# A two-layer encoder step on one core: two sums of weight blocks moved from VectorE to accumulating DMAs

## The reference, cut to what matters

```
def swiglu(x, w_gate, w_up, w_down):
    return (jax.nn.silu(x @ w_gate) * (x @ w_up)) @ w_down
...
x = x + 0.5 * swiglu(rms_norm(x, g_norm[l, 0]), w_ffn_gate[l, 0], w_ffn_up[l, 0], w_ffn_down[l, 0])
```

## Time and profile before

| | |
|---|---|
| median of 3 runs | 2529.57 us (2527.84 to 2533.5) |
| profiled execution: its time, its span | 2533.5 us, 2531.5 us |
| PE busy | 2422.3 us |
| DVE busy | 1932.6 us |
| ACT busy | 1337.9 us |
| POOL busy | 358.6 us |
| bytes moved by DMA | 300.90 MB |

### The profile page before, as it was taken

The page is one execution under the profiler, slowest core; times in us unless marked ns, Lnnn a source line. Parts: engine busy times, 40 slices in busy tenths (PEclk is TensorE's granted clock), DMA queues, the critical chain, the costliest instruction groups (busy, mean ns, idle before and its releaser), DMA issues. The chain is left out here.

```text
span 2531.5 us, 48940 instructions
## 1 busy us (share of the span) xinstructions
PE 2422.3 (96%) x18377; PEld 2273.4 (90%) x18377; DVE 1932.6 (76%) x3856; ACT 1337.9 (53%) x2870; POOL 358.6 (14%) x275
## 2 busy tenths in 40 slices
PE   8999999999998999999999999999999999999998
PEld 8999999788678999999988899999996699999998
DVE  7988989422697899898935889888928878888875
ACT  6555556201785655555522555555618756555554
POOL 0111111244000110111034011111031000111100
PEclk9999999999999999999999999999999999999999
DMA  4445353232763343445334554544357642544432
GB/s 128 108 91 117 87 118 80 85 117 84 276 245 106 76 117 85 112 97 112 71 87 135 150 115 96 113 98 106 82 207 256 221 114 60 124 102 103 108 84 79
DMA packets 352037, 300.90 MB, mean 119 GB/s; under 512 B 18305, under 2 KB 312378, under 8 KB 351554
## 3 DMA queue, kind: packets, MB, share of 16 engines
q1 hardware_dynamic: 279376, 246.98, 31.3%
q0 software_dynamic: 65776, 32.52, 10.5%
q10 hardware_dynamic: 6658, 18.37, 2.0%
HBM read 281.69 MB, written 16.13 MB: 118 GB/s over the span
## 5 line engine op out<-in xcount | busy, mean ns | idle before, releaser
L914 PE MATMUL PS<-x_area,w_area 128*128 128x320 f32 x3096 | 485.1, 310 | 0.0
L914 PEld LDWEIGHTS PS<-x_area,w_area 128*128 128x128 f32 x3096 | 461.1, 188 | 3.1 <-ACT PS L1710 2.9
L1625 ACT ACTIVATE w_area<-R 128x512 fp32r<-128x512 f32 (+2 forms) x583 | 322.7, 567 | 184.4 <-DVE R L2290 92.0
L2263 DVE TENSOR_TENSOR w_area<-R,w_area 128x512 fp32r<-128x512 f32 (+2 forms) x583 | 354.6, 617 | 67.8 <-ACT w_area L1625 67.3
L2263 DVE TENSOR_TENSOR r_area<-R,r_area 128x512 fp32r<-128x512 f32 (+2 forms) x437 | 270.7, 620 | 111.1 <-ACT r_area L1625 101.3
L914 PE MATMUL PS<-r_area,w_area 128*128 128x320 f32 x1584 | 268.3, 313 | 20.0 <-ACT PS L1710 12.6
L1625 ACT ACTIVATE r_area<-R 128x512 fp32r<-128x512 f32 (+2 forms) x437 | 248.4, 569 | 67.4 <-DVE R L2290 39.1
L2290 DVE TENSOR_TENSOR R<-R 128x512 f32<-128x512 f32 (+2 forms) x433 | 266.9, 616 | 1.0 <-DMA R<-in_w_ffn_gate_dram 0.7
L914 PEld LDWEIGHTS PS<-r_area,w_area 128*128 128x128 f32 x1584 | 241.3, 189 | 27.0 <-ACT PS L1710 23.7
L1710 ACT ACTIVATE PS<-PS 128x320 f32<-128x320 f32 x438 | 178.2, 416 | 163.6 <-PE PS L914 151.3
L1137 PE MATMUL PS<-w_area,xn_hi 128*128 128x512 f32 x800 | 253.5, 398 | 4.8 <-POOL w_area L771 3.5
(11 more groups left out here) (338 smaller groups left out, 3955.1 us busy)
## 6 DMA issues: line engine op xcount, KB each, us to landing
R<-in_w_ffn_up_dram SPq DMA_DIRECT2D x45, 512.0 KB, 4.0
R<-in_w_ffn_gate_dram SPq DMA_DIRECT2D x43, 512.0 KB, 4.0
R<-in_w_ffn_up_dram SPq DMA_DIRECT2D x86, 256.0 KB, 3.8
R<-in_w_ffn_gate_dram SPq DMA_DIRECT2D x82, 256.0 KB, 3.9
R<-in_w_ffn_down_dram SPq DMA_DIRECT2D x52, 384.0 KB, 3.1
R<-in_w_ffn_down_dram SPq DMA_DIRECT2D x88, 192.0 KB, 3.0
vreg<-in_cache_a_v_dram SPq DMA_DIRECT2D x8, 2048.0 KB, 9.0
...
```

The source lines that it names most:

```text
L914: last = pe.matmul(PS[:, bank, 0:HT], a[:, k, :], b, start=(start and opens), stop=(k == n - 1 and a is lo), skip_group_check=True)
L1625: act.activation(role_parts(f, g, s, role)[0], role_source(f, g, s, role), ACT.Copy).then_inc(sem("early_cast") if key in EARLY_COUNT else ...
L2263: dve.tensor_tensor(lo, role_source(f, g, s, role), hi.bitcast(F32), ALU.subtract).then_inc(sem("early_split") if key in EARLY_COUNT else ...
```

## The change

S3 is made by an accumulating DMA of GpSimd: W21 from DRAM is added over W11 in place (`third_sum`), after S2's sum and W11's low part have read it. S4 of gate and up sets is made so too: W12 is added over S2 in `sums` (`fourth_sum`), after S2's low part; S4 of down sets stays on VectorE. GpSimd's order is third(at), first(then), fourth(at). The cast and the low part of S3 move from the set itself to the end of the set before. The quarters go: one load brings W11 and W21, after S3's low part of the set two before, and `first_sum` waits for it. What is not shown is the bookkeeping of counts and the removal of the first S3 sums ahead of the chains.

```diff
--- before.py
+++ after.py
...
@@ -122,8 +122,8 @@
     order = chain(f)
     out = [(order[0], role) for role in ("W11", "S1", "S2", "W12", "S3")]
     for at, then in zip(order, order[1:] + [None]):
-        out += ([(then, "W11")] if then else []) + [(at, "S4")] + ([(at, "S3")] if at != order[0] else [])
-        out += ([(then, "S1"), (then, "S2")] if then else []) + [(at, "W22")] + ([(then, "W12")] if then else [])
+        out += ([(then, "W11")] if then else []) + [(at, "S4")] + ([(then, "S1"), (then, "S2")] if then else [])
+        out += [(at, "W22")] + ([(then, "W12"), (then, "S3")] if then else [])
...
             if j in own:
@@ -204,10 +204,7 @@
             if not early:
                 self.halves[p] += 1
                 self.landed2[key] = 16 * self.halves[p]
-                parts = ((1, "S3"), (2, "W22"), (3, "S2")) if (g, s) in order else ((1, "W21"), (2, "W22"), (3, "W21"))
-                if (g, s) in order:
-                    self.landed3[key] = 16 * len(self.landed3) + 16
-                for part, last in parts:
+                for part, last in ((1, "S3" if (g, s) in order else "W21"), (2, "W22")):
                     self.raw_free[key, part] = self.raws.get((p, part), 0)
                     self.raws[p, part] = self.split[f, g, s, last]
...
 
-            def quarter_load(f, g, s):
-
-                key, p = (f, g, s), LOAD[f, g, s] % 2
-                if PLAN.raw_free[key, 3]:
-                    sp.wait_ge(w_split, PLAN.raw_free[key, 3])
-                if PLAN.landed3[key] > 16:
-                    sp.wait_ge(w_loaded3, PLAN.landed3[key] - 16)
-                sp.dma_start(role_source(*key, "S1"), weight_block(*key, 0, 1)).then_inc(w_loaded3, 16)
-                if PLAN.raw_free[key, 1]:
-                    sp.wait_ge(w_split, PLAN.raw_free[key, 1])
-                sp.dma_start(role_source(*key, "W11"), weight_block(*key, 0, 0)).then_inc(w_loaded[p], 16)
-                set_load(f, g, s, (1,))
-
             def cols(w, slot, at, kb=KB):
                 return (raw[slot][:, 0:kb * P].rearrange("p (k m) -> p k m", k=kb),
                         w[:, bass.ds(at, P)].rearrange("(k p) m -> p k m", p=P))
@@ -620,7 +603,7 @@
                     load_constants()
                 for g, s in chain(f):
                     if set_at(f, g, s) is not early:
-                        quarter_load(f, g, s)
+                        set_load(f, g, s)
...
             def add_sums(f):
 
                 def first_sum(at):
-                    key = (f, *at)
+                    key, p = (f, *at), LOAD[(f, *at)] % 2
                     if key not in PLAN.first_added:
                         return
-                    pool.wait_ge(w_loaded3, PLAN.landed3[key])
-                    if PLAN.first_added[key] > 16:
-                        pool.wait_ge(sem("first_added"), PLAN.first_added[key] - 16)
+                    pool.wait_ge(w_loaded[p], PLAN.landed[key])
+                    pool.wait_ge(sem("first_added"), PLAN.first_added[key] - 16) if PLAN.first_added[key] > 16 else None
                     pool.dma_start(role_source(*key, "S1"), weight_block(*key, 1, 1), accum_op=ALU.add).then_inc(sem("first_added"), 16)
 
+                def third_sum(at):
+                    key = (f, *at)
+                    pool.wait_ge(w_summed, PLAN.sum[(*key, "S2")])
+                    if (*key, "W11") not in EARLY_COUNT:
+                        pool.wait_ge(w_split, SPLIT[(*key, "W11")])
+                    pool.wait_ge(sem("third_added"), PLAN.third_added[key] - 16) if PLAN.third_added[key] > 16 else None
+                    pool.dma_start(role_source(*key, "S3"), weight_block(*key, 0, 1), accum_op=ALU.add).then_inc(sem("third_added"), 16)
+
+                def fourth_sum(at):
+                    key = (f, *at)
+                    if key not in PLAN.fourth_added:
+                        return
+                    if (*key, "S2") in EARLY_COUNT:
+                        pool.wait_ge(sem("early_split"), EARLY_COUNT[(*key, "S2")])
+                    else:
+                        pool.wait_ge(w_split, SPLIT[(*key, "S2")])
+                    pool.wait_ge(sem("fourth_added"), PLAN.fourth_added[key] - 16) if PLAN.fourth_added[key] > 16 else None
+                    pool.dma_start(role_source(*key, "S4"), weight_block(*key, 1, 0), accum_op=ALU.add).then_inc(sem("fourth_added"), 16)
+
                 order = chain(f)
-                for at in order:
-                    first_sum(at)
+                first_sum(order[0])
+                for at, then in zip(order, order[1:] + [None]):
+                    third_sum(at)
+                    if then is not None:
+                        first_sum(then)
+                    fourth_sum(at)
...
                     act.wait_ge(sem("first_added"), PLAN.first_added[f, g, s])
+                elif role == "S3":
+                    act.wait_ge(sem("third_added"), PLAN.third_added[f, g, s])
+                elif role == "S4":
+                    act.wait_ge(sem("fourth_added"), PLAN.fourth_added[f, g, s])
...
@@ -1774,12 +1783,12 @@
                 role_high(f, *then, "W11")
                 role_high(f, *cur, "S4")
                 hidden_rows(f, *prev, "4")
-                role_high(f, *cur, "S3")
                 role_high(f, *then, "S1")
                 copy_rows(f, *cur, 2)
                 role_high(f, *then, "S2")
                 role_high(f, *cur, "W22")
                 role_high(f, *then, "W12")
+                role_high(f, *then, "S3")
...
@@ -1802,7 +1811,6 @@
                     role_high(f, *cur, "S4")
                     if n:
                         rows_on(f, *prev, 0)
-                        role_high(f, *cur, "S3")
...
                             copy_rows(f, *then, 1)
+                        role_high(f, *then, "S3")
...
 
             def role_sum(f, g, s, role):
                 key, p = (f, g, s), LOAD[f, g, s] % 2
-                a, b = {"S1": ("S1", "W22"), "S2": ("S1", "W11"), "S3": ("S2", "W22"), "S4": ("S4", "W12")}[role]
-                if role == "S3":
-                    dve.wait_ge(w_summed, PLAN.sum[(*key, "S2")])
-                    if (*key, "W11") in EARLY_COUNT:
-                        dve.wait_ge(sem("early_split"), EARLY_COUNT[(*key, "W11")])
-                    else:
-                        dve.wait_ge(w_split, SPLIT[(*key, "W11")])
-                if role != "S2" and set_at(f, g, s) is early:
+                a, b = {"S1": ("S1", "W22"), "S2": ("S1", "W11"), "S4": ("S4", "W12")}[role]
+                if role == "S1" and set_at(f, g, s) is early:
                     dve.wait_ge(sem("early_loaded"), 32 if f == 1 else 64)
                 elif role == "S1":
-                    dve.wait_ge(w_loaded3, PLAN.landed3[key])
+                    dve.wait_ge(w_loaded[p], PLAN.landed[key])
                     dve.wait_ge(w_loaded2[p], PLAN.landed2[key])
                 elif role == "S2" and (*key, "S1") in PLAN.sum:
                     dve.wait_ge(w_summed, PLAN.sum[(*key, "S1")])
-                    if set_at(f, g, s) is not early:
-                        dve.wait_ge(w_loaded[p], PLAN.landed[key])
                 elif role == "S2":
                     dve.wait_ge(sem("first_added"), PLAN.first_added[key])
-                    dve.wait_ge(w_loaded[p], PLAN.landed[key])
                 else:
                     dve.wait_ge(w_loaded2[p], PLAN.landed2[key])
                 at = (role_source(f, g, s, x) for x in (role, a, b))
-                dve.tensor_tensor(*at, ALU.subtract if role == "S3" else ALU.add).then_inc(w_summed, 1)
+                dve.tensor_tensor(*at, ALU.add).then_inc(w_summed, 1)
...
@@ -2555,16 +2554,15 @@
                 role_low(f, *then, "W11")
                 role_low(f, *cur, "S4")
                 hidden_lows(f, *prev, "4")
-                role_low(f, *cur, "S3")
                 dve.wait_ge(w_split, SPLIT[(f, *cur, "S4")])
                 role_sum(f, *then, "S2")
                 role_low(f, *then, "S1")
                 role_low(f, *then, "S2")
-                role_sum(f, *then, "S3")
                 fifth_rows(f, *cur)
                 role_low(f, *cur, "W22")
                 first_rows(f, *cur)
                 role_low(f, *then, "W12")
+                role_low(f, *then, "S3")
...
@@ -2578,7 +2576,8 @@
                     after_up, after_gate = inner and prev[1] % 2 == 1, inner and prev[1] % 2 == 0
                     plain = (f, cur[0]) in PLAIN
                     turned = after_up and not plain
-                    role_sum(f, *cur, "S4")
+                    if is_down(*cur):
+                        role_sum(f, *cur, "S4")
...
@@ -2588,8 +2587,6 @@
                     role_low(f, *cur, "S4")
                     if turned:
                         hidden_sums(f, *prev, ("5", "7", "6"))
-                    if n:
-                        role_low(f, *cur, "S3")
                     if then is not None:
```

22 lines of the change are left out of this document (9 added, 13 removed).

## The result

The changed kernel takes 2645.1 us (median of 4 runs, 2639.5 to 2650.8) against 2528.7 us of the kernel before on the same chip: 1.046 times as long, 95% interval 1.043 to 1.049. The profiled execution took 2654.3 us.

A forecast was written before the change was run, and what follows sets the result against it. TensorE was taken as the bound, busy 96%, with only its idle time to win. Gains of 39 + 6 + 1 us less 6 for late adds made 40 us, from 2529.6 (median) to 2490 us; range 2470 to 2555.

The forecast's parts named there:

- TensorE is the bound and only its idle time can be won: Whole kernel: TensorE busy 96% of the span, at most 109 us idle to win; three-pair group expected at about 112.2 us.
- The opening down set: First down set of a group, using hidden rows just made: 3.4 us lost, of which 2.5 us was expected back.
- one gain of 3.5 us: Per three-pair group: 0.77 after an up set, 2.5 at the opening down set, 0.2 before the up set's W22.
- My sign against that: Sign of a wrong chain: the cast of hidden rows "5" at an opening still waits over 3 us for VectorE.
- VectorE's relief: VectorE loses 146 S3 and 86 S4 operations, 143 us of its 1932.6; pays only where VectorE is late.
- my 46 us for place and relief: Gains summed: 39 us in eleven three-pair groups, 6 in four two-pair groups, 1 at the first part's start.
- The loads cost nothing, cover about 5 us: One half load replaces two quarters in 143 sets; it takes about 4 us of a 12.3 us set, costed at nothing.
- The S3 adds are covered, thinly: S3's adds land before ScalarE's cast can use them; a late one has 2 to 3.5 us before TensorE needs the copy.
- The S4 add lands after 6.4 us, 6 us subtracted: S4's add, third in GpSimd's queue, lands after 6.4 us; 6 us over the run subtracted for late adds.
- The circle bears 6.65 us, break-even at 7.5: Loop over buffer sums (S2 sum, low part, add, S4 cast, low part) sustains 6.65 us landings; 7.5 cancels the 3.5 won.
- rival 1: Adds become the bound at S4's cast in gate and up sets; landing of 8.0 gives 2567 us; chance 0.18, 2545 and more.
- My test for the failure: Wrong if ScalarE's w_area casts wait for GpSimd's DMA (covers), or if GpSimd adds' median landing is over 7.5 us.

The follow-up runs named there:

- place_only: Kernel before with only S3's cast and low part moved to the end of the set before, quarter loads and VectorE sums kept; 2498.4 us, 0.990 of before.
- no_adds: Changed kernel without GpSimd's third and fourth adds and without VectorE sums in their place, so operands hold other numbers; 2490.4 us, 0.986 of the kernel before.
- no_fourth: Changed kernel without GpSimd's fourth add (S4 of gate and up sets takes S2's sum as it is), third adds kept; 2532.0 us, 1.003 of the kernel before.
- thin_third: Changed kernel with the third add cut to a quarter of its bytes, all waits and queue places kept; 2533.9 us, 1.003 of the kernel before.

## Why the prediction was wrong, step by step

- **TensorE is the bound and only its idle time can be won**: right. The three-pair group fell to 112.8 us and 111.7 without the adds; I had said 112.2.
- **The opening down set**: right in kind. In the group of the kernel before, stalls of 0.77, 1.41 and 1.15 us stand; in place_only only one of 1.36 is left, in the place of the 1.41. S3's low part was the cause of the last one, and removing it from there needs none of the offloading. I had put it down as part of one gain of 3.5 us; the place alone gives 2.7. In no_adds the 1.36 falls to 0.23, so the opening chain does come forward with VectorE's relief. My sign against that (the cast of the hidden rows still waits over 3 us) was a bad one: it waits 3.8 us there and in the kernel after.
- **VectorE's relief**: my 46 us for place and relief, less the load's 20, would be 26; no_adds gained 34 net. Slightly too small.
- **The loads cost nothing, cover about 5 us**: wrong by 20 us. The cover held in three-pair groups (112.7 and 112.8) and failed once in each part, in the last down sets of the two-pair group (about 4, 6, 5 and 1 us in the four parts), a place I had not read. Down sets there have depth 2, 42 matmuls or 6.2 us each, and not the 12.3 us that my cover of about 5 us was reckoned from.
- **The S3 adds are covered, thinly**: wrong by 42 us. A three-pair group pays little, 0.3 us in the table and some 1.2 with its 6 missing matmuls reckoned in. Most lies at the openings of the parts (7.2 us in one stall of no_fourth, beside the stores) and in their last down sets. There the 2 to 3.5 us that I had given ScalarE behind a late S3 cast are taken by norm work that stands ahead of the copies.
- **The S4 add lands after 6.4 us, 6 us subtracted**: this step failed the forecast. It lands after 8.8. I had let each of two adds in front delay it by 0.8 us (2.1 us of transfer less 1.28 of issue); the delay is 2.2 and 2.0 us. One part of the error is shown: GpSimd's issues follow each other 0.75 and 0.87 us apart (medians), not 1.28, since an issue starts before the one ahead has ended. By my own rule that would give 4.8 + 1.35 + 1.23 = 7.4 us, already near the break-even. The other 1.4 us stay open; loads that cross the adds and the longer issue are candidates. That the bytes in front count is shown by thin_third: a third add with three quarters less of them, 1.6 us of transfer, brings the fourth add forward by 1.5 us. This rung costs 113 us, where I had put the adds' lateness at 6.
- **The circle bears 6.65 us, break-even at 7.5**: not contradicted (7.3 harmless, 8.8 not, nothing tried between), and rival 1 was the case. In the round shown the circle takes 4.98 us beside the landing, where I had 5.65 on average. I priced it at a landing of 8.0, 2567 us. With 8.8 and its own formula the excess is 6 x 2.15 - 1.7 = 11.2 us a group, 7.7 net; 13 groups make 100 us, from 2529 to some 2630. With 8.5, the median of the whole run, it is 77 us and 2606. So that 2630 comes near 2645 is in part luck: the formula has neither the other two wrong covers nor the lower clock.
- **My test for the failure** stood in the text. ScalarE's casts into w_area do wait for GpSimd's DMA. The other half, a median landing of GpSimd's adds over 7.5 us, came true of the fourth adds alone (8.5); the page has 6.4, 6.9 and 5.3 us for adds of all kinds in gate, up and down sets. The test should have named the fourth adds. The q0 share of 50% in gate sets was right (1200 to 1260), and so were VectorE's 209 sums:

```profile
q0 software_dynamic: 7291, 3.63, 49.4%
q1 hardware_dynamic: 4638, 4.60, 24.9%
```

So the traffic was foreseen and its effect on the third add in a row was not. The chance of 0.18 for rival 1 rested on today's adds landing within 5.3 us, but these never had another add in flight beside them.

The rule of the Trainium skill that I had weighed, DMA: Bandwidth & Descriptors (the anatomy of one DMA from gpsimd), 2.0 us plus the bytes at 436 KB per us, would be 2.15 us for 64 KB and 2.6 for 256 KB, both as estimates from the page. The runs show 2.6 and 4.6 us: near it for the small add, far from it for the large, and the measurement decides.
